# An MoE layer's expert bias: from products on TensorE to rows written into the PSUM banks ahead of the products

## The reference, cut to what matters

```python
h = xb @ w_up[e] + b_up[e]
g = jnp.minimum(h[:, :D_FF], SWIGLU_LIMIT)
lin = jnp.clip(h[:, D_FF:], -SWIGLU_LIMIT, SWIGLU_LIMIT)
act = g * jax.nn.sigmoid(SWIGLU_ALPHA * g) * (lin + 1.0)
return act @ w_down[e] + b_down[e]
```

## Time and profile before

| | |
|---|---|
| median of 3 runs | 2232.03 us |
| the runs | 2227.58 to 2233.63 us |
| the profiled execution | 2227.35 us |
| its span | 2225.6 us |
| mean granted clock of TensorE in it | 0.982 |
| HBM traffic over the span | 260 GB/s |

### The profile page before, as it was taken

How to read it: one execution, slowest core, us unless ns; L and a number is a source line. 1 busy time by engine, 2 the same in 40 slices (tenths; PEclk the granted TensorE clock), 3 DMA queues, 4 the chain that set the end, 5 groups by cost and what they waited for, 6 DMA issues and landing times.

```text
span 2225.6 us, 33282 instructions
## 1 busy us (share of the span) xinstructions
PE 2126.1 (96%) x10402; PEld 1765.4 (79%) x10403; DVE 1610.5 (72%) x1858; ACT 1211.4 (54%) x1251; POOL 587.9 (26%) x589
## 2 busy tenths in 40 slices
PE   7999987997899999999999999999999999999996
PEld 6887987686588888888888878887888888878785
DVE  4688977447855665778698675977976887677766
ACT  4423262331545554666577564757755676565655
POOL 1001031106511111334053050513511252131404
PEclk9999999997899999999999999999999999999998
DMA  7123275512976765979699795988986898777967
GB/s 186 58 86 139 86 164 190 185 57 86 351 260 215 226 223 179 338 246 373 228 359 378 233 331 180 362 284 286 364 310 224 284 369 308 244 244 282 309 238 271
DMA packets 287303, 541.66 MB, mean 243 GB/s; under 512 B 37302, under 2 KB 53798, under 8 KB 286146
## 3 DMA queue, kind: packets, MB, share of 16 engines
q1 hardware_dynamic: 262866, 495.07, 63.9%
q0 software_dynamic: 24368, 45.72, 8.2%
HBM read 513.61 MB, written 65.13 MB: 260 GB/s over the span
## 4 chain that ended last, share of the span: by engine, by line
PE 55%; issue 6%; DVE 6%; ACT 3%; DMA 3%; ACTq 0%; DVEq 0%; POOL 0%; SPq 0%; POOLq 0%
PE ex_ps_l L2945 7%; PE ex_ps_l L2944 7%; PE ex_ps_g L2944 6%; PE ex_ps_g L2945 6%; PE ex_ps_y L2944 5%; PE ex_ps_y L2945 5%; PE ex_ps_l L2948 4%; PE ex_ps_g L2948 4%; PE ex_ps_y L2948 3%; DVE ex_w_lo L2711 3%; PE ex_ps_t L2882 2%; ACT ex_w_hi L2579 2%; DMA ex_late<-in_w_down_dram 2%; PE ex_ps_t L2892 2%; PE ex_ps_g L2954 1%
## 5 line engine op out<-in xcount | busy, mean ns | idle before, releaser
L2711 DVE TENSOR_TENSOR ex_w_lo<-ex_late,ex_w_hi 128x2048 fp32r<-128x2048 f32 x204 | 464.2, 2291 | 222.5 <-ACT ex_w_hi L2579 154.7
L2411 POOL TENSOR_TENSOR ex_passed<-keep_ident 128x1 f32<-128x1 f32 x136 | 125.7, 924 | 1102.2 <-ACT ex_y L2622 1077.9
L2579 ACT CAST ex_w_hi<-ex_late 128x2048 fp32r<-128x2048 f32 x170 | 324.5, 1909 | 115.7 <-PE ex_ps_g L2945 60.7
L2711 DVE TENSOR_TENSOR ex_w_lo<-keep_sig_o,ex_w_hi 128x2048 fp32r<-128x2048 f32 x136 | 309.6, 2288 | 100.1 <-ACT ex_w_hi L2579 100.1
L2579 ACT CAST ex_w_hi<-keep_sig_o 128x2048 fp32r<-128x2048 f32 x134 | 255.1, 1904 | 120.6 <-PE ex_ps_l L2945 37.0
L2944 PE MATMUL ex_ps_l<-ex_w_hi,ex_x_hi 128*128 128x512 f32 x784 | 308.6, 394 | 2.0 <-DVE ex_w_lo L2711 2.0
L2944 PE MATMUL ex_ps_g<-ex_w_hi,ex_x_hi 128*128 128x512 f32 x784 | 306.5, 391 | 3.8 <-DVE ex_w_lo L2711 2.1
L2945 PE MATMUL ex_ps_l<-ex_w_lo,ex_x_hi 128*128 128x512 f32 x784 | 305.5, 390 | 0.0
L2945 PE MATMUL ex_ps_g<-ex_w_lo,ex_x_hi 128*128 128x512 f32 x784 | 305.1, 389 | 0.0
L2944 PE MATMUL ex_ps_y<-ex_w_hi,ex_h_hi 128*128 128x512 f32 x544 | 217.3, 400 | 1.2 <-DVE ex_h_lo L2747 0.9
L2945 PE MATMUL ex_ps_y<-ex_w_lo,ex_h_hi 128*128 128x512 f32 x544 | 212.1, 390 | 0.0
(11 more groups left out here) (507 smaller groups left out, 4114.2 us busy)
## 6 DMA issues: line engine op xcount, KB each, us to landing
keep_sig_o<-in_w_up_dram SPq DMA_DIRECT2D x102, 1024.0 KB
ex_late<-in_w_up_dram SPq DMA_DIRECT2D x102, 1024.0 KB
ex_late<-in_w_down_dram SPq DMA_DIRECT2D x102, 1024.0 KB
keep_weights<-in_w_up_dram SPq DMA_DIRECT2D x68, 1024.0 KB
keep_sig_o<-in_w_down_dram SPq DMA_DIRECT2D x34, 1024.0 KB
st_tab<-tabs SPq DMA_DIRECT2D x8, 1408.0 KB, 12.4
keep_weights<-in_w_in_dram SPq DMA_DIRECT2D x5, 1024.0 KB, 5.5
pr_late_pieces<-in_w_in_dram SPq DMA_DIRECT2D x5, 1024.0 KB
```

The source lines that it names most:

```text
L2411: pool.tensor_tensor(passed[:, :], ident[:, 0:1], ident[:, 0:1], ALU.add).then_inc(passed_done, 1)
L2579: nc.scalar.copy(w_hi[:, j % SPLIT, :, :], raw(j)).then_inc(hi_done, 1)
L2711: v.tensor_tensor(w_lo[:, j % SPLIT, :, :], raw(j), w_hi[:, j % SPLIT, :, :].bitcast(F32), ALU.subtract).then_inc(lo_done, 1)
```

## The change

The products on line 2954 go, and with them `pick`, `choose`, `choose_second`, `row_pick`, `bias_hl` and its making. In their place each bank of `w_up` is written by ScalarE with the bias (and the linear one with the bias plus 1) before its first product, and no product of `w_up` has `start=True` any more. The bias is at that time in `bias`, 128 x 2048, the expert's row spread over all partitions. For that, GpSimd loads 8 KB per pass and issues four `partition_broadcast` of 512 columns each. In a pass with a small second block the lower 64 rows of its banks are seeded with zero through `one_above`.

Where it all stands: GpSimd, in pass n, between the gather for pass n + 1 and the scatter of pass n, waits for ScalarE to have read pass n's last linear quarter and broadcasts pass n + 1's row. ScalarE in a pass of one block seeds three banks after chunk 3's cast and the fourth (`seed_first`, for the next pass) at j = 10; in a pass of two blocks it seeds `ps_g[1]` before chunk 3's cast, both `ps_l` after it, both `ps_g` again at j = 2, both `ps_l` again at j = 4, and the next pass's first at j = 10. TensorE waits for the seeds at chunks 0, 2, 4 and 6.

```diff
@@ GpSimd @@
+                def spread_bias(n, turn):
+                    pool.wait_ge(passed_done, turn)
+                    if n is None:
+                        pool.wait_ge(first_bias_in, 16)
+                    else:
+                        pool.wait_ge(bias_in, n * 16)
+                        pool.wait_ge(l_seeded, n * 2)
+                    pool.tensor_tensor(spread[0:16, :], ident[0:16, 0:1], ident[0:16, 0:1], ALU.add).then_inc(spread_go, 1)
+                    for part, half in ((0, 0), (1, 0), (0, 1), (1, 1)):
+                        q = 2 * part + half
+                        pool.partition_broadcast(bias_quarter(part, half), bias_row[:, q * 512:(q + 1) * 512]).then_inc(bias_spread, 1)
...
-                def scatter(n, at, second, turn, blocks):
+                def scatter(n, at, second, turn, blocks, spread_to):
                     for b in range(PAIR):
                         pool.wait_ge(y_free[b], n * 16 + 16)
+                    pool.wait_ge(bias_spread, n * QUARTERS + spread_to)
                     pass_on(turn)
...
+                        pool.wait_ge(bias_spread, n * QUARTERS + QUARTERS)
                         pass_on(n * 4 + 2)
+                        load_bias(pool, pool.snap(e + 1 - follows), bias_in)
...
                         gather(n + 1, after, pool.snap(after + 1 + skip), n * 4 + 3)
+                        spread_bias(pool.snap(n + 1), n * 4 + 4)
...
                 gather(0, 0, pool.snap(three_blocks(first_plan) + 1), 1)
+                spread_bias(None, 2)
+                pool.wait_ge(bias_spread, QUARTERS)
+                pool.memset(one[:, :], 1.0).then_inc(ones_set, 1)
+                pool.memset(one_above[0:SMALL, :], 1.0).then_inc(ones_set, 1)
+                pool.wait_ge(ones_set, 2)
+                pool.memset(one_above[SMALL:P, :], 0.0).then_inc(ones_set, 1)
@@ ScalarE @@
+                def seed_g(bank, half, above=False):
+                    scale = one_above[:, 0:1] if above else 1.0
+                    return nc.scalar.activation(bank[:, :], bias_quarter(0, half), ACT.Copy, scale=scale)
+
+                def seed_l(bank, half, above=False):
+                    plus = one_above[:, 0:1] if above else one[:, 0:1]
+                    scale = one_above[:, 0:1] if above else 1.0
+                    return nc.scalar.activation(bank[:, :], bias_quarter(1, half), ACT.Identity, bias=plus, scale=scale)
+
+                def seed_first(n):
+                    act.wait_ge(bias_spread, n * QUARTERS + 1)
+                    seed_g(ps_g[0], 0).then_inc(g_first_seeded, 1)
...
+                    act.wait_ge(bias_spread, n * QUARTERS + QUARTERS)
+                    if blocks == 2:
+                        act.wait_ge(y_b_read, n + 1)
+                        seed_g(ps_g[1], 0, small).then_inc(g_seeded, 1)
+                    if kind is not ALONE:
                         hi(n, SPLIT - 1, True)
+                    if blocks == 2:
+                        seed_l(ps_l[0], 0)
+                        seed_l(ps_l[1], 0, small).then_inc(l_seeded, 1)
+                    else:
+                        act.wait_ge(y_b_read, n + 1)
+                        seed_l(ps_l[0], 0).then_inc(l_seeded, 1)
+                        seed_g(ps_g[1], 1).then_inc(g_seeded, 2)
+                        seed_l(ps_l[1], 1).then_inc(l_seeded, 1)
                     for j in range(CHUNKS):
+                        if blocks == 2 and j == 2:
+                            act.wait_ge(glu_done, n * 10 + 3)
+                            seed_g(ps_g[0], 1)
+                            seed_g(ps_g[1], 1, small).then_inc(g_seeded, 1)
+                        if blocks == 2 and j == 4:
+                            act.wait_ge(lin_read, n * 4 + 2)
+                            seed_l(ps_l[0], 1)
+                            seed_l(ps_l[1], 1, small).then_inc(l_seeded, 1)
...
+                        if kind is AHEAD and j == 10:
+                            act.wait_ge(glu_done, n * 10 + 7)
+                            seed_first(n + 1)
...
-                act.wait_ge(h3_out, 16 * TT)
-                act.wait_ge(bias_plus, 1)
-                nc.scalar.copy(bias_hl[0:2 * E, :], bias_rows[0:2 * E, :]).then_inc(bias_hi_set, 1)
+                act.wait_ge(primed, 1)
+                act.wait_ge(ones_set, 3)
+                seed_first(0)
                 hi(0, 2, False)
@@ VectorE @@
-                def choose(n, e):
-                    v.tensor_copy(pick[:, 0, :], keep["row_pick"][:, bass.ds(e, 1)].to_broadcast([P, P])).then_inc(pick_set, 1)
...
-                v.wait_ge(bias_in, 32)
-                v.tensor_scalar(bias_rows[0:2 * E, F:2 * F], bias_rows[0:2 * E, F:2 * F], 1.0, None, ALU.add).then_inc(bias_plus, 1)
...
-                v.tensor_tensor(bias_hl[E:2 * E, :], bias_rows[E:2 * E, :],
-                                bias_hl[E:2 * E, :].bitcast(F32), ALU.subtract).then_inc(bias_set, 1)
@@ TensorE @@
+                    if j == 0:
+                        if first_part:
+                            pe.wait_ge(g_first_seeded, n + 1)
+                        else:
+                            pe.wait_ge(g_seeded, n * 2 + 1)
+                    elif j == 4:
+                        pe.wait_ge(g_seeded, n * 2 + 2)
+                    elif j in (2, 6):
+                        pe.wait_ge(l_seeded, n * 2 + (j // 4 + 1))
...
-                            first = kk == 0
-                            last = (not up) and part == 1 and k == 3
+                            first = kk == 0 and not up
+                            last = part == 1 and k == 3
...
-                            col = (j // 2) % 2 * F + (j // 4) * 512
-                            mm = pe.matmul(to[:, :], pick[:, b, :], bias_hl[:, col:col + 512], start=False, stop=True)
...
-                for _ in range(4):
-                    pe.matmul(ps_g[0][:, :].rearrange("p (a n) -> p a n", a=4), ident[:, :],
-                              ident[:, :].unsqueeze(1).to_broadcast([P, 4, P]), start=True, stop=True)
+                for seeded in ps_g + ps_l:
+                    mm = pe.matmul(seeded[:, :].rearrange("p (a n) -> p a n", a=4), ident[:, :],
+                                   ident[:, :].unsqueeze(1).to_broadcast([P, 4, P]), start=True, stop=True)
+                mm.then_inc(primed, 1)
```

More of the change, by code:

```diff
@@ L2519, in one_pass @@
                     else:
-                        scatter(n, own, second, n * 4 + 4, blocks)
+                        scatter(n, own, second, n * 4 + 4, blocks, 2 * QUARTERS)
                 pass_on(None)
@@ L2712, in lo, with x_low @@
                                     w_hi[:, j % SPLIT, :, :].bitcast(F32), ALU.subtract).then_inc(lo_done, 1)
[L2714 to L2720 removed]
+                def x_low(n, kind, blocks, b, i, small=False):
                     for half in range(2):
[L2722 to L2723 removed]
                         v.wait_ge(t_hi, turned(n, kind, blocks, i + half))
@@ L2816, in item @@
                             y_fold(n, j, blocks)
-                        if j == 9 and kind is AHEAD:
-                            choose(n + 1, e_next)
                         if j + SPLIT < CHUNKS or (kind is AHEAD and j < CHUNKS - 1):
@@ L2852, in later @@
                     n = v.snap(n)
-                    choose(n, e)
                     for j in range(SPLIT):
```

110 lines of the change are left out of this document (50 added, 60 removed).

## The result

The changed kernel takes 2361.28 us (median of 4 runs, 2358.99 to 2369.67) where the kernel before took 2231.31 us: a ratio of 1.060 (1.058 to 1.062). The prediction was 2215 us, within 2202 to 2243, with 0.22 for slower. It was wrong in sign and far outside its range: 130 us slower, not 16 us faster.

A forecast was written before the change was run, and what follows sets the result against it. TensorE was taken as the bound, with VectorE close behind in one-block passes. -27.3 + 8 + 3 = -16.3 us from 2227.35 gave 2211; 4 us more for later runs gave 2215, range 2202 to 2243.

The forecast's parts named there:

- part 3: GpSimd's load, addition and four broadcasts per pass: room enough, but broadcasts delay VectorE's splits; +8 us, bounds 2 to 18.
- part 4: The start: first product 3.3 us later, at 580.8; +3 us, between 1 and 7; possibly 6 us more, once, for a library.
- Part 1: TensorE's 196 bias products go, 44.6 us; the 27.3 us in 15 two-block passes count in full, 1.82 us each.
- Part 2: One-block passes: VectorE's chain, delayed by seeds, uses up the 17.3 us; no gain, 0.1 us lost each.
- Part 3's holds: Broadcasts of 0.8 us keep shared SBUF ports and delay VectorE's splits: 0.45 us per one-block pass, 8 us.
- rival (c): Slower: broadcasts of 2 us each hold VectorE in one-block passes; +43 us, 2274 us; chance 19%.
- (d): Seeds in two-block passes come after the products want them, so the 27.3 us become waits; +11 us, 2243; chance 5%.

The follow-up runs named there:

- e1: Changed kernel with GpSimd's one-column additions in the expert loop replaced by copies, except in the last pass: 2246.32 us, ratio 1.011 to the kernel before.
- e3: Kernel before plus one unread 8-column broadcast a pass behind GpSimd's gather, which brings both gaps: 2228.42 us, ratio 1.0036.
- e9: Kernel before with copies for GpSimd's one-column additions except in the last pass, plus four unread 128x512 broadcasts a pass: 2229.08 us, ratio 1.0034.
- e11: Kernel before with all additions kept, plus four unread 128x512 broadcasts a pass, so both gaps stay; no seeds: 2374.13 us, ratio 1.065.
- e2: Changed kernel without row loads and broadcasts, biases of `w_up` left out, so the seeds alone: 2221.71 us, ratio 1.0000 to the kernel before.
- e5: e2 with the three seeds at the head of a one-block pass moved apart on ScalarE: 2208.53 us, ratio 0.9937 to the kernel before.
- e6: e1 with the three seeds at the head of a one-block pass moved apart on ScalarE: 2221.4 us, ratio 0.9998 to the kernel before.
- e8: e6 plus one 8-column broadcast at the end of GpSimd's part of the stage before: 2216.18 us, ratio 0.9974 to the kernel before.
- e7: Kernel before with four unread 128x512 broadcasts a pass; additions made copies except the last pass's and the one before the gather's transfers: 2291.81 us, ratio 1.032.

## Why the prediction was wrong

**The step that failed** is part 3 with its aside in part 4. Part 3 says "Each pass adds one 8 KB load, one small addition and four broadcasts" and "GpSimd is busy 16.47 of 36.08 us, so there is room even for 4 x 2 us". The load of a library was named in part 4 as a possible 6 us, "once". It comes twice a pass, 68 times in all, at 6.8 to 10.5 us, because each pass alternates between the addition and the broadcast. And the room was taken from the busy share of a whole pass, when what counts is the stretch between the end of the gather and ScalarE's request: 15.1 us, of which the change fills 26.4. Part 3 says that the scatter's preparation "has until ScalarE's first `y`", but no number was put on it. The trace of the kernel before had it, on ScalarE's timeline in the pass of the earlier trace rows:

```profile
1815.63 0.69 ACT L2622 ACTIVATE ex_y<-ex_ps_y,ex_scatter_at 128x512 f32<-128x512 f32 x1 [0.92 <-PE ex_ps_y L2948]
```

ScalarE was ready for it at 1814.71, 15.4 us behind the gather's end at 1799.35. The addition and the broadcasts alone would have fitted there (10.6 us); with the two gaps they don't. This is shown by e1 (105 us less without the gaps) and by e3, e9 and e11 (7.5 us for the gaps, 6.6 for the broadcasts, 147 for both).

**Part 1** had the mechanism right and the size too large. Two-block passes were to win 1.82 us each. They won 1.3 (59.00 to 57.68 us; 19.9 to 20.2 us in 15 passes in e1, e2 and e5, for 27.3). The eight products go at 0.227 us each; what is missing is a slower pitch in `w_down`, 0.233 us instead of 0.227 over its 80 or 96 products, which is 0.5 us. Two starts in e5 that lie five products apart, TensorE's timeline:

```profile
1947.35 0.39 PE L2998 MATMUL ex_ps_l<-ex_w_hi,ex_h_hi 128*128 128x512 f32 x1
...
1948.51 0.40 PE L3003 MATMUL ex_ps_l<-ex_w_hi,ex_h_lo 128*128 128x512 f32 x1
```

Five products in 1.16 us; at the same place before they took 1.13. Why is not settled; no run varied it. In the changed kernel only six of the 15 two-block passes show the gain; the other nine all stand behind a one-block pass, whose late `y` takes it from them.

**Part 2** had the right engine as the bound, and the wrong loss and the wrong wait. It gave a one-block pass +0.1 us. With the seeds where the change puts them (e2) it was +0.44 in a row, and +1.6 behind a two-block pass (14.1 / 9), a case that the prediction did not look at: it followed one pass in which ScalarE had time at the start. That VectorE's chain allows no gain was half right: with the seeds out of its way (e5) the passes in a row mostly win 0.4 to 0.5 us of the 0.91. The wait that was to take the gain, TensorE's for `hidden`, hardly grew: 9.4 us in 18 waits in e2 and 10.3 in e5 (600 to 2180 and to 2160 us), 11.5 before, where 1.3 us each were forecast. In e2 TensorE waited for VectorE's `h_lo` instead, 14.6 us in 16 waits, and for ScalarE's seed, 10.7 us in 7.

**Part 3's holds** were well sized. Of four undisturbed broadcasts in a row each takes 0.70 us (0.8 taken), of four beside the splits 2.0; first at the start and then in the second pass of those shown (GpSimd's timeline):

```profile
588.05 2.79 POOL L2420 PARTITION_BROADCAST ex_bias<-ex_end_rows  x4 [9.12 <-issue]
...
1960.44 8.01 POOL L2420 PARTITION_BROADCAST ex_bias<-ex_end_rows  x4 [8.27 <-issue]
```

8 us was the term, and e9 shows 5.9 us over the 33 passes (first products 572.18 and 2170.86, before 577.54 and 2170.30). So the condition of rival (c), 2 us per broadcast, was nearly met (1.65 us in the mean of the changed kernel, 1.70 in e9), and its price of 43 us was not: a broadcast is long mostly beside the splits, and lengthens them by 0.46 us at most. The rule of the Trainium skill (SBUF — State Buffer, "Who interferes with whom") agrees in direction: the longest split in e9 is 2750 ns, against 2295. No split was held for the whole length of a broadcast, 0.80 us at the least.

**Part 4** gave the first product at 580.8; it ran at 591.99. Of the 11.2 us between them 9.12 are the gap in front of the first broadcast, and 2.6 are that GpSimd got there later, at 578.9 and not 576.3. e6 and e5 put that gap and its broadcasts at 7.6 us.

**The rivals.** None was the cause. (c) has the right sign, and had 19%; its mechanism, holds of VectorE, was shown by e9 to cost 6.6 us. A reader who had chosen it would have had the sign by luck. (d), seeds too late, did come true, but in one-block passes. No rival asked what else an instruction that GpSimd had not used before could bring with it in every pass.

## What to carry to other kernels

On GpSimd, an operation of a kind that the loop did not have can cost a library load on each side of it, and the cost is a gap before an instruction, not the instruction: look in GpSimd's queue for `MODIFY_POOL_CONFIG` and keep each loop within one library (a copy did for the addition here). Room on an engine is not its idle share of a pass but the stretch between its last release and the next request for it: measure that, and add up everything that is to stand in it. Two additions that are cheap apart (7.5 and 6.6 us here) can cost ten times their sum together (147 us), when together they are longer than the stretch. A copy of half a microsecond on a half-idle engine costs nothing or 1.6 us a pass, depending on what is queued around it at the turn from one pass to the next.

## What the runs showed of the hardware

- A library change costs 6.8 to 10.5 us on GpSimd in the changed kernel, 5.8 us at the least in e8 and e11 and 12.6 us at the most in e7. In e9 the pair of `MODIFY_POOL_CONFIG` still runs ahead of the broadcasts in 33 passes, but from the second such pass on the gap is 0.1 to 0.2 us: the library is there already. The Trainium skill (GPSIMD Engine Reference, "Instruction dispatch") has about 6 us for the first call to a freshly loaded kernel. The shortest gaps here are of that size (5.82 us in e8), and the usual ones are longer.
- GpSimd's four broadcasts of 128x512 take 2.79 us alone and 8.01 or 8.78 us beside VectorE's splits; the splits grow from 2.29 to at most 2.75 us.
- TensorE's clock went to 0.50 after many of the waits of the changed kernel (behind a stand of 8.61 us for the 5.7 us of the window shown), and is 1.00 in the two-block pass shown in which it never waits. Its mean is 0.956 over the span, that of the kernel before 0.982.
